# Feature-major selection of expert rows, and the last tile's router logits moved ahead of other selections

## The reference, cut to what matters

```python
x = x + merged @ w_out
h = rmsnorm(x, g_ffn)
lg = h @ w_rg + b_rg                     # 4 groups: top-1
le = (h @ w_re).reshape(..., 4, 8) + b_re  # 8 experts in the group: top-2
gate = ...                               # softmax weights, zero for the others
y = 0
for e in range(32):
    hid = silu(h @ w_e1[e]) * (h @ w_e3[e])   # 1024 -> 256
    y = y + gate[..., e:e+1] * (hid @ w_e2[e])  # 256 -> 1024
x = x + y
```

## Time and profile before

| | |
|---|---|
| time, median of 3 runs | 634.83 us (634.35 to 634.88) |
| the profiled execution: its own time | 635.66 us |
| its span in the trace | 633.8 us |
| granted TensorE clock, mean of the span | 0.994 |
| PE busy | 609.9 us (96%) |
| DVE / ACT / POOL busy | 291.0 / 186.5 / 149.2 us |
| read from memory | 147.12 MB |

### The profile page before, as it was taken

How to read it: one execution, slowest core, us unless ns; L and a number is a source line. 1 busy time by engine, 2 the same in 40 slices (tenths; PEclk the granted TensorE clock), 3 DMA queues, 4 the chain that set the end, 5 groups by cost and what they waited for, 6 DMA issues and landing times.

```text
span 633.8 us, 9981 instructions
## 1 busy us (share of the span) xinstructions
PE 609.9 (96%) x3746; PEld 378.8 (60%) x3746; DVE 291.0 (46%) x813; ACT 186.5 (29%) x582; POOL 149.2 (24%) x341
## 2 busy tenths in 40 slices
PE   8999999999999999999999999999999999978895
PEld 7888867677456667666677767854443444434341
DVE  3343947757883589772043321675133133131302
ACT  5524224532478444423100101121221121112201
POOL 1596727733584525410000000000000000000000
PEclk9999999999899999999999999999999999989999
DMA  9793543222300343322479991099999999999993
GB/s 293 188 292 116 193 166 100 68 67 85 113 2 33 115 152 100 100 67 100 152 224 403 401 394 48 9 400 384 420 420 420 420 419 418 420 421 421 420 412 124
DMA packets 57715, 150.57 MB, mean 238 GB/s; under 512 B 12352, under 2 KB 40448, under 8 KB 45760
## 3 DMA queue, kind: packets, MB, share of 16 engines
q1 hardware_dynamic: 57664, 149.89, 63.2%
HBM read 147.12 MB, written 2.76 MB: 236 GB/s over the span
## 4 chain that ended last, share of the span: by engine, by line
PE 92%; DVE 3%; issue 2%; ACT 2%; DMA 1%; SPq 0%; POOL 0%; DVEq 0%
PE PS L835 28%; PE PS L845 21%; PE PS L1232 10%; PE PS L1126 7%; PE PS L1271 6%; PE PS L1261 5%; PE PS L961 2%; PE PS L918 2%; PE PS L1183 2%; PE PS L986 2%; PE PS L828 1%; PE PS L1028 1%; PE PS L969 1%; PE PS L907 1%; DMA X<-in_x_prompt 1%
## 5 line engine op out<-in xcount | busy, mean ns | idle before, releaser
L835 PE MATMUL PS<-hT,W 128*128 128x320 f32 x416 | 117.2, 436 | 0.0
L835 PEld LDWEIGHTS PS<-hT,W 128*128 128x128 f32 x416 | 77.6, 190 | 33.4 <-issue 3.8
L1232 PE MATMUL PS<-E,xT 128*32 128x256 f32 (+1 forms) x1088 | 62.8, 382 | 8.2 <-issue 7.9
L1232 PEld LDWEIGHTS PS<-E,xT 128*32 128x32 f32 x1088 | 35.9, 110 | 34.8 <-issue 15.4
L2209 POOL TENSOR_SCALAR means<-sums 128x4 f32<-128x4 f32 (+3 forms) x35 | 7.7, 221 | 187.9 <-ACT junk L1371 186.9
L1126 PE MATMUL PS<-h,S 128*128 128x512 f32 (+1 forms) x96 | 48.2, 625 | 0.3 <-DVE S L1999 0.3
L845 PE MATMUL PS<-W,hT 128*128 128x256 f32 (+5 forms) x256 | 41.7, 353 | 0.0
L1271 PE MATMUL PS<-yb,WG 128*128 128x512 f32 (+1 forms) x96 | 38.5, 609 | 0.8 <-DVE yb L2124 0.8
L845 PEld LDWEIGHTS PS<-W,hT 128*128 128x128 f32 (+1 forms) x256 | 31.5, 163 | 8.4 <-issue 1.3
L845 PE MATMUL PS<-W,mergedT 128*128 128x384 f32 (+3 forms) x192 | 35.7, 381 | 0.0
L835 PE MATMUL PS<-uT,W 128*128 128x320 f32 x128 | 34.6, 432 | 0.0
(11 more groups left out here) (316 smaller groups left out, 984.5 us busy)
## 6 DMA issues: line engine op xcount, KB each, us to landing
E<-in_w_e SPq DMA_DIRECT2D x93, 1024.0 KB, 23.0
W<-in_w_in SPq DMA_DIRECT2D x7, 1536.0 KB, 7.1
W<-in_w_in SPq DMA_DIRECT2D x7, 1024.0 KB, 8.1
W<-in_w_mem_kv SPq DMA_DIRECT2D x4, 1024.0 KB, 6.9
W<-in_w_glu SPq DMA_DIRECT2D x4, 768.0 KB, 8.2
W<-in_w_out SPq DMA_DIRECT2D x2, 1536.0 KB, 15.7
X<-in_x_prompt SPq DMA_DIRECT2D x4, 512.0 KB, 4.6
W<-in_w_o_mem SPq DMA_DIRECT2D x1, 1536.0 KB, 6.9
```

What stands on the lines that cost most here:

```text
L835: ins = mm(out[:, 0:TOK], w[:, k, cols:cols + 128], rhs[:, k, :], start=(k == 0), stop=(k == kt - 1))
L1232: ins = mm(PS[r:r + B, AB, 128 * which.start:128 * which.stop], xT[:, k, place_ + B * n:place_ + B * n + B], E13[slot][:, which, k, j::2], ...
```

## The change

1. **Rows of a team in one product.** `x_products` takes h2 as the stationary operand (128 features at a step of 8, by tile) and S as the moving one (128 columns), and so writes the features-by-slots layout at once: 8 feature groups by 3 tiles, 24 products a team. `xg`, `row_copies`, `row_transposes` and the semaphores between them are gone. Odd pairs issue their 24 in three pieces: two feature groups before the transpose of hid, two behind it, four behind `down`.
2. **Order of PE at the end of the tail.** Between wout (0, 2) and the transposes of tile 2 stand two feature groups of tile 0 and the ranks of tile 1. The logits of tile 2 follow the transposes directly; the other selections, and the counts for the last ranks (`counted`), come behind them. `last_ranks` stands in front of `seed(0)`. Seed 3 moves to pair 0 behind `first_up`, seed 4 (with the signal `seeded`) in front of pair 0's `down`, seeds 1 and 2 to pair 2.
3. **Squares in two parts.** ACT squares columns 384 to 1023 of tile 2 after wout (1, 2), columns 0 to 383 after wout (0, 2); POOL adds the two sums in its scale-and-add instruction.
4. **DVE.** The experts of tile 1 come before the last `residual`; the first half of `h2` of tile 2 (four of each eight features) before the logits of tile 2, the second behind `homes`; the overflow table moves behind the y copies of pairs 1 and 3.
5. **SP.** The reload of the first two up slots stands before the wait for `seeded` and down 6. The slot of down 6 moves off tile 0 of `X`.

The diff, cut to its core:

```diff
--- before.py
+++ after.py
@@ -312,6 +312,7 @@
 
 SUMS = [(2, (0, 1)), (0, (0,)), (0, (1,)), (1, (0,)), (1, (1,))]
 LAST_K = 6
+LAST_COLS = 128 * DGROUPS[0][1]
 OV_STEPS = 3 + 6 + 1 + 2
 
 
@@ -729,14 +731,13 @@
             for e in range(4, UPS):
                 load_up(e)
 
-            sp.wait_ge(s["seeded"], 1)
-            sp.wait_ge(s["h2_ready"], NT + 1)
-            load_down(DOWNS - 1)
-
             for n, (sem_, value) in enumerate(((s["first_gates"], 1), (s["ab_full"], 1))):
                 sp.wait_ge(sem_, value)
                 for e in range(2):
                     sp.dma_start(E13[e][:, n], e13_src[n][:, e + UPS]).then_inc(up_loaded[e], 16)
+            sp.wait_ge(s["seeded"], 1)
+            sp.wait_ge(s["h2_ready"], NT + 1)
+            load_down(DOWNS - 1)
             for p in range(PAIRS):
                 ups, downs = (range(2 * p + n, min(2 * p + 2 + n, NE)) for n in (UPS, DOWNS))
                 if p > 0 and ups:
@@ -1100,6 +1101,8 @@
                 pe.wait_ge(s["onehot_ready"], 2)
                 mm(PS[:, YB, NE:2 * NE], const("upper"), both[:, 1, :], start=True, stop=False)
                 mm(PS[:, YB, NE:2 * NE], const("ones"), both[:, 0, :], start=False, stop=True).then_inc(s["rank_full"], 1)
+
+            def counted():
                 for t in range(NT - 1):
                     mm(PS[:, LAST_RANKS, 0:2 * NE], const("ones"), both[:, t:t + 1, :].broadcast_to([128, 2, NE]), start=(t == 0), stop=False)
 
 
-            def tile_rows(banks, t, c):
-                n = TILES[t][1]
-                return mm(PS[:, banks + c, :], S[0:n, t, :], h2[0:n, t, 512 * c:512 * c + 512], start=(t == 0), stop=(t == NT - 1))
-
-            def rows_done(banks, full):
-                for c in range(2):
-                    for t in range(NT):
-                        ins = tile_rows(banks, t, c)
-                    ins.then_inc(full, 1)
-
-            def choose_first(t, c):
+            def x_products(bank_, h, ks, ts):
+
+                for k in ks:
+                    for t in ts:
+                        n = TILES[t][1]
+                        ins = mm(PS[:, bank_, 128 * (k % 4):128 * (k % 4) + 128], h2[0:n, t, k::KD], S[0:n, t, :],
+                                 start=((k, t) == (4 * h, 0)), stop=((k, t) == (4 * h + 3, NT - 1)))
+                return ins
+
+            def x_half(h):
+                return range(4 * h, 4 * h + 4)
+
+            def choose_first(t, h, ks=None):
                 pe.wait_ge(s["chosen"], t + 1)
-                pe.wait_ge(s["h2_ready"], t + 1 + (c if t == NT - 1 else 0))
-                ins = tile_rows(ROWS, t, c)
+                pe.wait_ge(s["h2_ready"], t + 1 + (h if t == NT - 1 else 0))
+                ins = x_products(ROWS + h, h, ks or x_half(h), (t,))
                 if t == NT - 1:
-                    ins.then_inc(s["rows_full"], 1)
-
-            def choose(g):
-                pe.wait_ge(s["chosen"], g + NT)
-                pe.wait_ge(s["weights_ready"], g)
-                pe.wait_ge(s["y_dve"], 2 * g - 1)
-                pe.wait_ge(s["y_act"], 2 * g - 1)
-                rows_done(ROWS, s["rows_full"])
+                    ins.then_inc(s["xt_full"], 1)
+
+            def choose(g, h, ks):
+                if ks[0] == 0:
+                    pe.wait_ge(s["chosen"], g + NT)
+                    pe.wait_ge(s["weights_ready"], g)
+                elif ks[0] == 4:
+                    pe.wait_ge(s["xt_ready"], 2 * g + 1)
+                ins = x_products(ROWS, h, ks, range(NT))
+                if ks[-1] % 4 == 3:
+                    ins.then_inc(s["xt_full"], 1)
 
             for kind, *which in TAIL:
                 if kind == "wout":
@@ -1153,43 +1161,25 @@
                                 s["merged"] if (kind, g, t) == TAIL[0] else None)
                 elif kind == "yT":
                     if which[0] == NT - 1:
-                        choose_first(0, 0)
+                        choose_first(0, 0, (0, 1))
+                        next_ranks()
                     rows_turned(*which)
                     if which[0] == 1:
                         first_ranks()
-                    if which[0] == NT - 1:
-                        next_ranks()
-                        choose_first(0, 1)
                 else:
                     route(*which)
-            for c in range(2):
-                choose_first(1, c)
+            choose_first(0, 0, (2, 3))
+            choose_first(0, 1)
+            counted()
+            for h in range(2):
+                choose_first(1, h)
+            last_ranks()
             emptied(LAST_WOUT[NT - 1])
             seed(0)
-            last_ranks()
-            seed(1)
-            seed(2)
-            for c in range(2):
-                choose_first(2, c)
-            emptied(("route", NT - 1))
-            seed(3)
-            seed(4).then_inc(s["seeded"], 1)
+            for h in range(2):
+                choose_first(2, h)
             pe.wait_ge(s["emptied_dve"], sum(1 for _, w in UNITS if w == "dve"))
             pe.wait_ge(s["emptied_act"], sum(1 for _, w in UNITS if w == "act"))
-
-            def row_transposes(h, bank_, full):
-
-                for k in range(4):
-                    ins = nc.tensor.transpose(PS[:, bank_, 128 * k:128 * k + 128], xg[:, 4 * h + k::KD], ident)
-                ins.then_inc(full, 1)
-
-            def x_transposes(g, h):
-
-                if h == 0:
-                    pe.wait_ge(s["rows_ready"], 2 * g + 2)
-                elif g > 0:
-                    pe.wait_ge(s["xt_ready"], 2 * g + 1)
-                row_transposes(h, ROWS if g > 0 else ROWS + h, s["xt_full"])
 
...
@@ -1290,32 +1278,36 @@
                         warming(ROWS, 512)
                 if p == 0:
                     first_up()
+                    seed(3)
                 else:
                     up(p)
+                if p == 2:
+                    seed(1)
+                    seed(2)
                 if p > 0 and p % 2 == 0:
                     add_team(p // 2 - 1, range(3))
                 elif p % 2 == 1 and p < PAIRS - 1:
-                    choose(p // 2 + 1)
+                    choose(p // 2 + 1, 0, (0, 1))
                 hid_transpose(p)
                 if p > 0 and p % 2 == 0:
                     add_team(p // 2 - 1, range(3, len(SUMS)))
                 elif p % 2 == 1 and p < PAIRS - 1:
-                    x_transposes(p // 2 + 1, 0)
+                    choose(p // 2 + 1, 0, (2, 3))
                 if p % 2 == 0:
                     spread(p // 2)
+                if p == 0:
+                    seed(4).then_inc(s["seeded"], 1)
                 down(p)
                 if p % 2 == 1 and p < PAIRS - 1:
-                    x_transposes(p // 2 + 1, 1)
+                    choose(p // 2 + 1, 1, x_half(1))
             add_team(TEAMS - 1, range(len(SUMS)))
 
             with pe.If(teams > 0):
                 with pe.Fori(0, OV_TEAMS) as i:
                     pe.wait_ge(s["ov_chosen"], NT * i + NT)
@@ -1358,7 +1350,7 @@
                 return [st.mark(fn(dst[:, part], src[r:r + n, 0:part.stop - part.start], ACT.Copy),
                                 s["emptied_act"] if part.stop == dst.free_size() else None) for r, part in parts]
 
-            def sumsq(key, srcs, *after):
+            def sumsq(key, srcs, *after, head=0, ready="sums_ready"):
 
                 n = norm_rows(key)
                 st.after(*after)
@@ -1368,8 +1360,8 @@
                     for m in {junk_at[q] for q in parts if junk_at[q]}:
                         st.after(m)
                     q = parts[0]
-                    ins = fn(junk[0:n, 256 * q:256 * q + w], src, ACT.Square, accum_out=sums[0:n, NORM_NO[key], h:h + 1])
-                    m = st.mark(ins, s["sums_ready"] if h == len(srcs) - 1 else None)
+                    ins = fn(junk[0:n, 256 * q:256 * q + w], src, ACT.Square, accum_out=sums[0:n, NORM_NO[key], head + h:head + h + 1])
+                    m = st.mark(ins, s[ready] if h == len(srcs) - 1 else None)
                     for q in parts:
@@ -1560,8 +1552,11 @@
                     act.wait_ge(*emptied_at(UNIT_NO["gluv", d - 2]))
                 empty(gsig[:, d % 2, :], src[:, 0:TOK], ACT.Tanh, scale=0.5)
             for t, (f, n) in enumerate(TILES):
+                if t == NT - 1:
+                    act.wait_ge(*emptied_at(UNIT_NO["wout", 1, t]))
+                    sumsq(("f", t), [X[0:n, t, LAST_COLS:D]], head=1, ready="rest_summed")
                 act.wait_ge(*emptied_at(UNIT_NO[LAST_WOUT[t]]))
-                sumsq(("f", t), [X[0:n, t, :]])
+                sumsq(("f", t), [X[0:n, t, 0:D if t < NT - 1 else LAST_COLS]])
                 for g in range(2):
...
@@ -1924,9 +1905,10 @@
                     st.mark(V_.scalar_tensor_tensor(x, src[r:r + n, 0:part.stop - part.start], 0.5, x, ALU.mult, ALU.add),
                             s["emptied_dve"] if part.stop == 128 * nd else None)
 
-            def normed(t, cols=slice(0, D)):
```

(57 more changed lines are left out.)

35 lines of the change are left out of this document (9 added, 26 removed).

## The result

The changed kernel takes **701.68 us** (701.15 to 703.36, 4 runs) against 634.86 us of the kernel before beside it (634.35 to 636.44, 4 runs): ratio 1.1052, 95% interval 1.1026 to 1.1079, 66.8 us slower. The forecast was 633.3 us, in a range of 632.4 to 635.1.

The account below looks back on a forecast made before the run. The weight stream at 420 GB/s was taken to bound the kernel: 635.66 - 1.86 (hole closed) + 0.3 (PE late at the end) = 634.1 us for the profiled execution, 633.3 us for the median, range 632.4 to 635.1.

Parts of the forecast that it names:

- What bounds the kernel: Expert stage: a stream of weights at a steady 420 GB/s sets the end; PE time saved mid-stage only lengthens stalls.
- The first term: Start of the expert stage: earlier `first_up` and half loads close the hole in the weight stream, 1.86 us less.
- I take 0.12 a record: New 128-column selection products: price taken from the router's records, 0.12 us a record, 0.24 a product.
- My upper end, 0.31: New selection products: a weight load of 0.192 that hides behind nothing plus a product of 0.12, 0.31 us a record.
- a bound from below: New selection products: a transpose of 128 columns takes no less than 0.1 us, so the record was put at 0.12.
- Rival (c): Start of the stage: weight loads don't hide, 44 selection records at 0.31 us; 5.5 us slower, 640.4; chance 0.07.
- All of it turns into stalls: Middle of the stage: 1.75 us less PE time in each of seven odd pairs becomes stalls from about pair 8 on.
- the second term, 0.3 us: Late pairs: a longer stall lowers the clock in pair 14, 1.2 us less 0.92 of stall, PE late by 0.3.
- The seeds that I had called free: Pairs 0 and 2: moved seeds, 1.0 us of PE each, cost nothing because slots are loaded ahead.
- The logits came earlier as forecast: Start of the stage: logits of tile 2 end at 414.1 instead of 415.45, 1.3 us earlier.
- 422.1: Start of the stage: `first_up` starts at 422.1 instead of 426.52.
- rival (a): Last pairs: the lower clock makes PE late, 0.5 to 1.5 us given back, say 634.3; chance 0.22.

Follow-up runs that it names:

- Experiment 3: Kernel before with only SP's edit: the wait for `seeded` and down 6 moved behind the four half loads; 636.06 us, ratio 1.0028.
- experiments 8 and 9: Kernel before with 512-column products that feed nothing ahead of each odd pair's selection: four in 8, 649.06 us (1.0230); one in 9, 634.45 us (0.9999).
- experiment 4: Changed kernel with h2 laid out by feature groups and tile 2 padded to 128 rows; 633.17 us, ratio 0.9974 against the kernel before.
- experiment 2: Kernel before with series of products that feed nothing ahead of w_out, at operand steps 1, 2, 4 and 8; 0.112, 0.118, 0.233, 0.238 us a record.
- experiment 6: Changed kernel with tile 2 padded to 128 rows, step of 8 kept; 659.01 us, ratio 1.0379 against the kernel before.
- experiment 1: Changed kernel with h2 laid out by feature groups, so the stationary operand has no step; 635.66 us, ratio 1.0018 against the kernel before.
- experiment 5: Kernel before with series that feed nothing, heights 128, 128, 64 in turn or 64 alone, steps 1 and 8; at step 1, 0.173 us a record in turn, 0.112 alone.
- 7: Changed kernel without its selection: old 512-column products, xg and transposes, overflow table unmoved, the rest as changed; 635.82 us, ratio 1.0008 against the kernel before.
- experiment 10: The kernel with feature groups and tile 2 padded to 128 rows run again, unchanged; 633.30 us, ratio 0.9975 against the kernel before.

## Why the prediction was wrong

**What bounds the kernel** was right. Experiment 3 lost by the stream what its hole grew, and experiments 8 and 9 found PE's room. The first term (1.86 us) was a term of a kernel in which the new products are cheap; in the execution of experiment 4 the hole is nearly closed, and the median is the one forecast, 633.2 against 633.3. That agreement is partly luck: this is another kernel, and its executions differ (632.51 with a hole of 0.2 us, 633.40 with 1.0).

**The step that failed is the price of a record**, "I take 0.12 a record", from router products. Those have a contiguous stationary operand and one height in a series. The new products lack the first everywhere and the second in the odd pairs. The step of 8 makes 0.12 into 0.24 (experiment 2), and the change of height makes that 0.30 (12 records in 3.63 us, at the full clock). My upper end, 0.31, was close to the right number by luck: I had added a load of 0.192 that hides behind nothing to a product of 0.12. The step instead makes the load itself longer, 328 ns; what in a change of height costs 0.19 us is not shown. The prediction gave the step no words. It took a transpose of 128 columns as a bound from below, and the transposes of xg read with the same step; experiment 2 shows that they don't pay for it (0.111) while products with either operand stepped do.

**The second failure is where the price was charged.** Rival (c) put 0.31 on the 44 records of the start alone and left the middle free: 5.5 us. "All of it turns into stalls" holds only below the budget. By the chains, from the first expert product to the last pair's: before, 189.3 us, of which 9.1 were stalls and lowered clock; after, 681.54 - 427.45 = 254.1. Worked out from the rows of the chains, the difference is

| | us |
|---|---|
| selection 15.1 instead of 7.95 (xg and transposes included), seven times | +50 |
| down 3.4 instead of 1.85, up 4.8 instead of 3.8, seven times | +18 |
| `first_up` 5.5 instead of 3.95 | +1.6 |
| four seeds moved behind `first_up`, 4.0, of which 1.1 fill a wait for hid in pair 0 | +2.9 |
| transposes of hid in odd pairs, before in the shadow of the copy to xg | +2 |
| stalls and lowered clock that were there before | -9 |
| sum, against 64.8 measured | +65.5 |

`first_up` comes 0.9 us later (427.45, 426.52 before) and the part behind the last pair's start is 0.3 longer: with the 64.8 that is 66.0, the difference of the two profiled executions; the medians differ by 66.8. The seeds that I had called free are in the sum as well: past the budget nothing is.

**The clock.** I looked for it behind stalls; the second term, 0.3 us, was of that kind. In the changed kernel it fell with no stall ahead, twice a team. In the middle of the stage this took both halves: no such dip with the step alone (experiments 2 and 6), none with the heights alone (experiment 1 between 430 and 594 us), but with both (the kernel itself, experiment 5). Both together also space the records furthest, 0.30 us, so no run tells the combination from the spacing. At the start of the stage neither half is needed: the clock fell in experiment 6 with the step alone, and in 1 (0.50 in 422 to 424), 7 and 10 without step or alternation. What of the products the chip goes by stays open.

**Padding and step are not additive.** From the changed kernel, taking away the step is worth 66.0 us and the padding 42.7; from there the other one is worth 2.5 and 25.8. The stream is the floor under both.

**The start.** The logits came earlier as forecast. In experiment 1 `first_up` came at 423.2, not 422.1, with the clock at 0.50 in 422 to 424; in experiment 4, at a full clock, 12.1 us behind SP's first issue, where the forecast had 11.7. The late last pair that rival (a) described appeared in experiment 1 (1.1 us slower than before) and in the execution of experiment 10, but not in that of 4: with the padding it depends on the execution. So the second term, 0.3 us, is neither shown nor refuted. The 7.55 us that I took for the old selection is 7.95 in the chain, since its eight transposes take 1.35 and not 1.0.

## What to carry to other kernels

Price an operand by its access pattern as well as its shape: a float32 matmul operand with a step of 4 or 8 elements doubled the record here, and each change of the number of rows between products added about 0.19 us. Store the rows in the order in which they will be loaded, and pad the odd tile; both are one edit. And before calling an engine's time free, work out its budget against the real bound, and hold the pessimistic end of every price against that budget over the whole loop, not only on the path at its start.

## What the runs showed of the hardware

- Stationary float32 operand, 128x128, 128 columns moving: 0.112 us a record at a step of 1 element, 0.118 at 2, 0.233 at 4, 0.238 at 8. Moving operand at a step of 8: 0.233. Transposes at a step of 8: 0.111.
- 128, 128 and 64 rows in turn: 0.173 us a record, against 0.112 for either height alone; 0.19 us a change of height.
- Records with a step of 8 take the same at either clock (0.238 and 0.239 us).
- The granted clock fell to 0.50 without a stall ahead when step and change of height came together (twice a team in the changed kernel, and in experiment 5). Whether it falls at the start of the stage differs between executions of the same kernel: at 1.00 in the execution of experiment 4, while in that of 10 the first 12 selection records took 2.67 us instead of 1.53.
